# Moving the start addresses of the weight rings and the activations in SBUF

## The reference

```
for l in range(2):
    shift, scale, gate = split(silu(c) @ w_ada[l] + b_ada[l], 3)        # and the same for c_ctx
    u  = (rms(x, norm_w[l]) * (1 + scale) + shift) @ w_in[l]            # 2048 x 6208, x and ctx
    x += gate * (heads(u) * silu(z)) @ w_out[l]
z  = rmsnorm(x) @ w_in_2                                                # 2048 x 12304
x += rmsnorm((sigmoid(m_a) * (y_a @ w_proj_a) + sigmoid(m_b) * (y_b @ w_proj_b)) @ w_out_2)
x += rmsnorm(attention(h @ wq, mem @ wk, mem @ wv) @ wo)
x += rmsnorm((gelu(conv(h @ w_up)[gate]) * conv(h @ w_up)[up]) @ w_down)
```

## Time and profile before

| | us |
|---|---|
| median of three runs | 3782.4 (3779.97 to 3782.77) |
| the profiled execution | 3781.98 |
| its span, first to last instruction | 3780.2 |
| TensorE busy | 3573.4 (95%) |
| VectorE busy | 2016.0 (53%) |
| ScalarE busy | 1671.3 (44%) |

### The profile page before, as it was taken

The page is one execution under the profiler, slowest core; times in us unless marked ns, Lnnn a source line. Parts: engine busy times, 40 slices in busy tenths (PEclk is TensorE's granted clock), DMA queues, the critical chain, the costliest instruction groups (busy, mean ns, idle before and its releaser), DMA issues.

```text
span 3780.2 us, 46318 instructions
## 1 busy us (share of the span) xinstructions
PE 3573.4 (95%) x18672; PEld 2944.7 (78%) x18672; DVE 2016.0 (53%) x3121; ACT 1671.3 (44%) x2722; POOL 68.0 (2%) x118
## 2 busy tenths in 40 slices
PE   7889999999998999999999999999999799999998
PEld 1667778878776777778877777866788699999887
DVE  1666654345567745643455544445455566666544
ACT  2323344434422424545644435445445654444443
POOL 1200000000020000000000000000000000000000
PEclk8999999999999999999999999999999899999999
DMA  9653312133365455323355566635656255565565
GB/s 361 199 157 112 106 56 56 52 110 110 102 182 173 146 179 178 90 67 108 104 190 162 162 181 180 189 108 163 187 175 200 90 180 183 184 184 182 190 203 171
DMA packets 351045, 577.49 MB, mean 153 GB/s; under 512 B 25316, under 2 KB 131060, under 8 KB 348912
## 3 DMA queue, kind: packets, MB, share of 16 engines
q1 hardware_dynamic: 344512, 549.47, 47.1%
q0 software_dynamic: 6320, 25.06, 2.3%
HBM read 570.26 MB, written 4.19 MB: 152 GB/s over the span
## 4 chain that ended last, share of the span: by engine, by line
PE 56%; DVE 4%; ACT 3%; DMA 2%; issue 1%; DVEq 0%; SPq 0%; ACTq 0%
PE ps L709 35%; PE ps L1604 13%; PE ps L1286 1%; DMA raw_ring<-in_w_in_dram 1%; ACT w_hi L672 1%; DVE w_lo L678 1%; PE ps L1198 1%; PE ps L1084 1%; PE ps L1171 1%; PE ps L1180 1%; PE ps L746 0%; PE ps L1477 0%; PE ps L1482 0%; PE ps L1194 0%; DMA raw_ring<-in_w_proj_b_dram 0%
## 5 line engine op out<-in xcount | busy, mean ns | idle before, releaser
L678 DVE TENSOR_TENSOR w_lo<-raw_ring,w_hi 128x1024 fp32r<-128x1024 f32 (+1 forms) x827 | 1010.1, 1223 | 1118.7 <-ACT w_hi L672 1117.7
L672 ACT CAST w_hi<-raw_ring 128x1024 fp32r<-128x1024 f32 (+1 forms) x827 | 863.9, 1047 | 1281.6 <-PE ps L709 523.5
L709 PE MATMUL ps<-w_hi,r_a 128*128 128x512 f32 x3552 | 1291.2, 403 | 61.4 <-DVE w_lo L678 19.4
L709 PE MATMUL ps<-w_lo,r_a 128*128 128x512 f32 (+1 forms) x2624 | 1029.1, 392 | 0.0
L709 PE MATMUL ps<-w_hi,r_b 128*128 128x512 f32 (+1 forms) x2272 | 851.0, 394 | 9.2 <-issue 4.4
L709 PEld LDWEIGHTS ps<-w_hi,r_a 128*128 128x128 f32 x3552 | 677.2, 191 | 229.3 <-issue 62.3
L709 PEld LDWEIGHTS ps<-w_lo,r_a 128*128 128x128 f32 x2624 | 501.8, 191 | 103.4 <-issue 7.9
L709 PEld LDWEIGHTS ps<-w_hi,r_b 128*128 128x128 f32 x2272 | 434.4, 191 | 103.4 <-issue 4.6
L1604 PE MATMUL ps<-r_a,w_hi 128*128 128x256 f32 x2816 | 508.9, 284 | 0.0
L1604 PEld LDWEIGHTS ps<-r_a,w_hi 128*128 128x128 f32 x2816 | 440.8, 193 | 0.0
L1604 PE MATMUL ps<-r_a,w_lo 128*128 128x256 f32 x1408 | 399.2, 284 | 0.0
(11 more groups left out here) (338 smaller groups left out, 2943.5 us busy)
## 6 DMA issues: line engine op xcount, KB each, us to landing
raw_ring<-in_w_in_dram SPq DMA_DIRECT2D x386, 512.0 KB, 3.7
raw_ring<-in_ffn_w_up_dram SPq DMA_DIRECT2D x176, 512.0 KB, 4.4
raw_ring<-in_w_ada_dram SPq DMA_DIRECT2D x128, 512.0 KB, 3.9
raw_ring<-in_w_out_dram SPq DMA_DIRECT2D x96, 512.0 KB, 3.7
raw_ring<-in_ffn_w_down_dram SPq DMA_DIRECT2D x88, 512.0 KB, 4.3
gla_arena<-in_w_ada_dram SPq DMA_DIRECT2D x64, 512.0 KB, 8.6
raw_ring<-in_w_proj_b_dram SPq DMA_DIRECT2D x32, 512.0 KB, 3.6
raw_ring<-in_w_proj_a_dram SPq DMA_DIRECT2D x16, 512.0 KB, 3.6
```

What stands on the lines that cost most here:

```text
L672: nc.scalar.copy(WH[:, ph.s_slot(i, j), 0:n], RAW[:, ph.raw_slot(i, j), 0:n]).then_inc(hi_ready, 1)
L678: nc.vector.tensor_tensor(WL[:, ph.raw_slot(i, j), 0:n], RAW[:, ph.raw_slot(i, j), 0:n], WH[:, ph.s_slot(i, j), 0:n].bitcast(F32), ALU.sub ...
L709: mm = nc.tensor.matmul(PS[:, t, a:z], X(x, k, t), W[w][:, kk * cols + a:kk * cols + z], start=(k == 0 and q == 0), stop=(c == len(js) - 1 ...
```

## The change

The five large buffers move within the slab. `raw_ring` and `w_hi` begin 192 bytes past a multiple of 512 (207040 and 194752, before 206848 and 194560). `r_a`, `r_b` with `gla_arena`, and `f_arena` with `act_t` begin 128 past one. The distance between `w_hi` and the end of `r_a` grows by 64 bytes. `vec_t` moves up by 192 bytes and `ada_t` down by 192; `b_ada_t` goes to the small tensors at the bottom, so that those placed after it move up by 384 bytes; `consts` stays. Nothing else is changed: same instructions, same order.

```diff
@@ -108,20 +108,20 @@
             return nc.alloc_sbuf_tensor_at(name, [P, words], dt, offset=offset)[:]
 
         big_end = (base + 53200 * 4) // 2048 * 2048
-        raw_off = big_end - 4 * RAW_SLOTS * SLOT
+        raw_off = big_end + 192 - 4 * RAW_SLOTS * SLOT
         hi_off = raw_off - 4 * SPLIT_SLOTS * SLOT
-        ra_off = hi_off - 4 * 8192
+        ra_off = hi_off - 64 - 4 * 8192
         rb_off = ra_off - 4 * 8192
         f_off = rb_off - 4 * 24832
         RAW = place("raw_ring", RAW_SLOTS * SLOT, F32, offset=raw_off).rearrange("p (s n) -> p s n", s=RAW_SLOTS)
         WL = place("w_lo", RAW_SLOTS * SLOT, F32R, offset=raw_off).rearrange("p (s n) -> p s n", s=RAW_SLOTS)
         WH = place("w_hi", SPLIT_SLOTS * SLOT, F32R, offset=hi_off).rearrange("p (s n) -> p s n", s=SPLIT_SLOTS)
         CN = place("consts", C_N)
-        VT = place("vec_t", 116, F32, offset=big_end)
-        BAT = place("b_ada_t", 96, F32, offset=big_end + 480)
+        VT = place("vec_t", 116, F32, offset=big_end + 192)
+        BAT = place("b_ada_t", 96)
         HG = place("head_gain", 16)
         SCT = place("silu_c_t", 32).rearrange("p (s k) -> p k s", s=2)
-        ADA = place("ada_t", LAYERS * 96, F32, offset=big_end + 864).rearrange("p (l f s) -> p l f s", l=LAYERS, s=2)
+        ADA = place("ada_t", LAYERS * 96, F32, offset=big_end + 672).rearrange("p (l f s) -> p l f s", l=LAYERS, s=2)
         AMUL = place("norm_mul", 32).rearrange("p (s k) -> p s k", s=2)
         GB = place("gain_rows", LAYERS * 268).rearrange("p (l n) -> p l n", l=LAYERS)
         NSINK = place("neg_sink", H_B)
@@ -148,7 +148,7 @@
         DEC = place("decay", 8).rearrange("p (t d c) -> p t d c", t=2, d=2)
         SSO = place("gla_sums", 8).rearrange("p (t h) -> p t h", t=2)
         RIO = place("gla_rinv", 8).rearrange("p (t h) -> p t h", t=2)
-        assert at[0] <= f_off and big_end + 864 + 4 * LAYERS * 96 <= base + 53200 * 4, at[0]
+        assert at[0] <= f_off and big_end + 672 + 4 * LAYERS * 96 <= base + 53200 * 4, at[0]
         RA = place("r_a", 8192, F32R, offset=ra_off)
         F = place("f_arena", 24832, F32, offset=f_off)
         RB = place("r_b", 8192, F32R, offset=rb_off)
```

## The result

The changed kernel takes 3799.07 us (median of 4 runs, 3791.76 to 3802.69) against 3781.49 us before: a ratio of 1.0043 with a 95% interval of 1.0029 to 1.0056, 17.6 us slower by the medians. The time lies in the forecast range, but the forecast was "no change", and the change is clear of noise.

What follows compares the result with a forecast made beforehand. The prediction took TensorE's weight matmuls, number times interval, to bound the kernel. Its terms for matmuls, VectorE and ScalarE, and transfers summed 0 + 0 + 0, so it forecast 3782.4 us, no change, range 3765 to 3830 us.

Steps and rivals of the forecast that it cites:

- What bounds the kernel: TensorE, busy 95% of the 3780.2 us span: the cost of a weight matmul times their number is the time.
- fixed part of 13.3 ns: Width-independent cost of each float32r weight matmul, 186 us over 14,016; taken as all an address could touch, bounding ±186 us.
- Step (a): Interval between float32r weight matmuls on L709 and L1604: no change, with 2.1 ns either way, 29 us, for the range.
- The kpe row: Matmuls on L746 with every second weight slice 256 bytes off: 24 take 5.54 us, like ordinary ones, so difference 0.
- The `consts` row: L1448's plain float32 matmuls, stationary operand 128 bytes past a multiple of 256: 0.60 against 0.59 us, at most some 10 ns.
- The glr row: Matmuls on L746 with 16-column weights at every 64 bytes: 117.9 ns, 2.1 ns less than L1604, perhaps because narrower.
- Rival 1: At each weight matmul's start, a moving operand inside an aligned block needs another fetch: +29 us, 3812 us, chance 0.20.
- Rival 3: On TensorE, weight load and moving operand collide today and the change separates them: 3773 or 3753 us, chance 0.14.
- Step (b): VectorE and ScalarE durations, chiefly the split of weight slots (1225 and 1047 ns): address costs 0, with slack as cover.
- Step (c): Transfers TensorE waits for, 140 us in front and later: landing times unchanged, 0, bound +17.5 us.
- rival 2: Transfers written off a multiple of 256 cost one piece more per row: up to +17.5 us, 3800 us, chance 0.11.
- The 8% of packet time on the source side: DMA engines spent 106 against 98 ns per packet on `w_in_2`'s unaligned source rows, with no landing time added.

Runs made afterwards that it cites:

- e1: Changed kernel with its activations back on a multiple of 512 and the rings still 192 bytes past one: 3816.22 us, ratio 1.0081 to before.
- e2: Kernel before with only the activations moved, to 128 bytes past a multiple of 512, rings on one: 3817.35 us, ratio 1.0092 to before.
- m2: Separate kernel of matmuls only, 48 per pair of operand offsets, no reference computed: float32r at distance 0 took 226.7 ns (512 columns) and 120.0 ns (256).
- f1: Kernel before with the up stage's activations alone 64 bytes lower, in a view of their own: 3748.57 us, ratio 0.9911.
- e3: Changed kernel with rings and activations both 128 bytes past a multiple of 512, so their distance is as before: 3790.38 us, ratio 1.0018.
- m4: Separate matmul-only kernel entering one distance from several others; fourth part alternated operand offsets in two orders: 231.6 and 231.7 ns there.
- m3: Separate kernel of transfers only, 64 loads of 512 KB per destination offset: 84.0 us at offset 0, 88.5 us at 128.
- g1: Changed kernel with the up stage's activations alone 64 bytes higher, at distance 0 to the rings: 3800.14 us, ratio 1.0057.

## Why the prediction was right or wrong

**What bounds the kernel** held for the largest terms: the number of weight matmuls times their interval. The bound on them held too: if the whole change is put down to the fixed part of 13.3 ns, it went to 20 ns in one case and to 6.6 in another. That it is the fixed part isn't shown: distance 64 adds 2.2 ns at 512 columns and takes 2.2 off at 256.

**Step (a), "I take 0", is the one that failed.** Measured: +2.2 ns (settled) on L709 up to the FFN, +6.6 on its last 1,056, -2.2 on L1604's 4,224. In the traces that is +9.7, +7.0 and -9.3 us. The gain on one line hides more than half of the loss on the other. That the time came out so near is luck: by the same argument each half of the change would have been forecast at 0, and they cost 33 and 34 us (e1, e2). The argument compared *offsets from a multiple of 512* and should have compared the *distance between the two operands modulo 256*:
- The kpe row was counted as nearest. Its weights are 256 bytes off, which is distance 0: it could not have shown anything. In the changed kernel its distance is 192, and it takes 5.65 us for 5.54; by the table 24 settled matmuls would take 0.16 us more, an estimate.
- The `consts` row is plain float32, which m2 shows at 429.2 ns whatever the distance (512 columns, four distances). The text saw that it might hide one, and then let it count anyway.
- The glr row, 117.9 ns where L1604 had 120.0, was the one float32r row of the trace whose weights run through distances other than 0, in steps of 64. It was explained away by its narrow operand, which no run tests. It gave the right sign for 256 columns. That it nearly gave the size (2.1 ns taken as a bound, 2.2 measured) is luck: in f1, at the same addresses, the same sum gives (5.63 - 0.28) / 47 = 113.8 ns.

**Rival 1** (slower, 3812 us) named the right place, the interval of the weight matmuls, and had the direction of L709's, but its mechanism is false: e1 and e2 show values away from before's with the moving operand aligned, e3 before's with it off. **Rival 3** was nearest: what counts is how the weights' address lies to the moving operand's, and for 256 columns it had the right sign. It took one sign for both widths. That the two reads collide, as it says, fits m2 but isn't shown by itself: the fourth part of m4, which was to look into it, told nothing. For 512 columns distance 0 is the best there is, and L709 has more than twice the matmuls.

**Step (b)** was right: 1225 and 1049 ns, within 2 ns of before, and the busy time of both engines is as before.

**Step (c) and rival 2**: the second term that was put at 0 and isn't. It is 2.4 us in front. With everything else that isn't the distance it is at most e3's 7.5 us (95% interval of the ratio 1.0006 to 1.0030, 2 to 11 us); the bound of +17.5 us was more than twice that. That the measured 3799 us lies beside rival 2's 3800 is a coincidence: the L709 and L1604 terms belong to another mechanism. The rule of the Trainium skill that spoke against the change ("DMA: Bandwidth & Descriptors", How a descriptor splits into AXI transactions) has a descriptor fetch, and pay for, the bytes below a start off 256 bytes; the estimate by it, 6% for 128 past, stands beside 5% that m3 measured on the side that is written. By the rule the cost grows with the offset (9% for 192), and m3 shows 5% for 4, 32, 64, 128 and 192 alike. The 8% of packet time on the source side, which the text held for the same effect, wasn't tested.

**The sum of the measured terms.** Between the two traces the intervals give +9.7 us (L709 before the up stage, 1.2 ns on the mean of 7,910, since its short runs of 24 hardly settle), -9.3 (up) and +7.0 (down): +7.4 us of a difference of spans of 16.1. The same count for the experiments:

| us more than before, in the traces | L709 before the up stage | up | down | sum | span |
|---|---|---|---|---|---|
| changed | +9.7 | -9.3 | +7.0 | +7.4 | +16.1 |
| e1 | +40.3 | -9.3 | +7.0 | +38.0 | +37.6 |
| e2 | +35.5 | -5.6 | +6.0 | +35.9 | +35.1 |
| e3 | 0.0 | 0.0 | 0.0 | 0.0 | +10.3 |
| g1 | +9.3 | 0.0 | +2.3 | +11.6 | +15.2 |

So the distance accounts for all of e1 and e2, and for less than half of the change itself. Much of the rest is what e3 pays as well, with its buffers off a multiple of 256 and the distance at 0: 7.4 us and e3's 7.5 are 14.9 of the measured 17.6. That the two simply add isn't shown: e1 and e2 have one kind of buffer off a multiple of 256 each, and their sums leave nothing for it (medians +33.3 and +34.4 us). Of e3's 7.5, 2.4 is the front, and 5% on the 49 us of later transfers on the chain is 2.5, an estimate from m3 and the earlier trace rows; what the remaining 2 to 3 us are is open. The columns of spans are single traces, and chance is of the same size: f1, at before's addresses up to the up stage, reached it 5.6 us earlier than before, and g1, at the changed kernel's addresses, 5.5 us earlier than the changed kernel. The clock has a part in it: TensorE was granted 1.2 GHz for 182.3 us of the changed kernel's trace against 164.1 us of before's, worth up to 9.1 us, but for 164.6 us of g1's. The four runs of the changed kernel had mean clocks of 0.974 to 0.979 of full speed, and the time followed them, 3802.69 us at 0.974, 3791.76 at 0.979. The runs of the kernel before, in the sets of the experiments, span 0.974 to 0.980, so no clear effect of the layout on the clock shows.

## What to carry to other kernels

Where float32r matmuls set the pace, look at the interval between starts, and at the distance modulo 256 bytes between the stationary and the moving operand: 512 columns want 0 (226.7 ns against 228.7 to 236.6 at every other distance tried), 256 columns one of the good distances (113.3 at 112, 113.3 or 117.8 at 192, against 120.0 at 0), and not just any: 80 and 96 bytes gave 120.0 as well, 4 and 8 bytes 123.3 and 126.7. Two buffers that both begin on a multiple of 256 are at distance 0, which is right for the one shape and wrong for the other; a view of its own for one stage's operand, with no instruction more, gave 0.9% here. Keep the buffers that transfers write on multiples of 256 bytes meanwhile (e3, m3). A row clears a suspected cost only if it varies the quantity that counts, at the rate that counts: ask of each comparison which other quantities it holds fixed.

## What was not expected of the hardware

- The interval of float32r matmuls depends on the distance of two operands that TensorE itself reads, with a period of 256 bytes, without any other engine at work (m2). The Trainium skill gives TensorE two independent SBUF read ports, one for the moving operand and one for the weight load ("SBUF — State Buffer", Who interferes with whom). The maps agree with its word that TensorE never waits on other engines, 226.7 and 120.0 ns with them and without; that the two reads don't affect each other doesn't fit 226.7 to 233.3 ns, wherever it is that they meet.
- Several settled patterns exist for one distance: 228.9 and 233.3 ns for 512 columns at 64, 117.8 and 113.3 for 256 columns at 192. A stage can keep one for its whole length, 1,056 matmuls, and the pattern can differ between two executions at the same addresses (the glr matmuls, 5.82 us in before and 5.63 in f1). What picks it is open.
- DMA destinations off a multiple of 256 bytes cost 5% at full rate, whether they are 4 or 192 bytes off (m3).
